# Gated rows turned by VectorE in 32x32 blocks, and down weights in runs of 16 KB

## The chip, the cores and the metric

The kernel runs on one core of a Trainium2 chip. The time is device time in microseconds (us). Three runs of the kernel before took 2269.36, 2270.11 and 2274.81 us; their median, 2270.11 us, is the time before. Engines are called PE (TensorE), DVE (VectorE), ACT (ScalarE), POOL (GpSimd) and SP (SyncE).

## The reference

One decoder layer over 1024 tokens of width 1024, all in float32. A mixer with three branches (a diagonal state-space model, a chunked spatial gating, cross-attention into 256 memory tokens) is followed by a routed mixture of experts, and then a last RMSNorm. The change is in the mixture of experts:

```python
g_idx = argmax(x @ w_group + b_group)            # 1 of 8 groups
top_vals, top_loc = top_k(e_logits[g_idx], 2)    # 2 of the 8 experts in it
# for each expert e, over the tokens that chose it:
y = (silu(xb @ w1[e]) * (xb @ w3[e])) @ w2[e]    # 1024 -> 512 -> 1024
```

There are 64 experts. w1 and w3 of one are 1024x512 (2 MB each), w2 is 512x1024 (2 MB).

## The kernel before

Up to about 1150 us the kernel computes the mixer, the router and a table that lists each expert's tokens. Then comes the expert stage. Its work is cut into units: a unit is up to 32 tokens (CAP) of one expert, and there are 100 of them in this run. `each_unit` (L382) writes the same loop for PE, ACT, DVE and POOL: over 16 turns, over 4 slots, over the units of expert 4t+s. The counts are read from `spans` at run time.

Weights: each of the 4 slots holds one expert, 6 MB. SP loads them in order of experts, all on one queue. `refill` (L548) waits until the last unit of the expert four back has done its gate and up projection (`gu_ready`), then issues the token list (L553), w1 and w3 (`expert_up`, L499; a partition takes 8 rows of 512 numbers that lie side by side, a run of 16 KB), waits for that unit's down projection (`y_ready`), and issues w2 (`expert_down`, L503; a partition takes rows p, 128+p, 256+p and 384+p, four runs of 4 KB each).

A unit u passes through the engines so:

- POOL (`gather`, L685) waits until PE has turned the rows of the unit before, copies 32 indices (L688) and gathers 32 rows of 4 KB from memory into `xg` (L692). There is one `xg`, so there is one gather at a time.
- PE turns the 32 rows (`turn_tokens`, L1031, transposes recorded at L758), DVE copies the result to `xT` (L1710).
- PE does the gate and up projection (L1045, 64 matmuls). The 512 hidden columns are in four quarters of 128: quarter h goes to partitions 32h to 32h+31, so a bank holds 128 partitions (quarter, token) by 128 columns. ACT makes silu of the gate (L1240), DVE multiplies with the up part into `hid` (L1715).
- PE turns the tokens of unit u+1 in between, then `hid` (128x128, L1052), and DVE copies it to `hidT` (L1717).
- PE does the down projection (L1059, 32 matmuls) against `w2s`, ACT drains the result (L1244) and stores it with four DMAs (L1247), 192 packets with their semaphore writes. There is one result row buffer for each slot, so the drain of the next unit in the same slot waits until the last store has landed (L1243).
- ACT's order is silu of u, drain of u, its four DMA issues, silu of u+1.

At the end the results are gathered, two rows for each token, and weighted and normed.

Of the kernel before, what the change touches and what calls it, by code (L numbers as in the profile page):

```python
# [27 lines left out]
ALU = mybir.AluOpType  # L28
# [3 lines left out]
P = 128  # L32
# [22 lines left out]
QUARTERS = P // CAP  # L55
# [48 lines left out]
def program(nc, x, mem, g_mix, g_mem, w_in, w_gate, b_gate, lam_re, lam_im, log_dt, b_re, b_im,  # L104
# [3 lines left out]
    with ctx:  # L108
        def sb(name, shape, dt=F32):
            return ctx.enter_context(nc.sbuf_tensor(name, shape, dt))  # L110

        def sem(name):
            return ctx.enter_context(nc.semaphore(name))


        act_bank = [ctx.enter_context(nc.psum_tensor(f"act_bank{i}", [P, 512], F32)) for i in range(4)]
        dve_bank = [ctx.enter_context(nc.psum_tensor(f"dve_bank{i}", [P, 512], F32)) for i in range(4)]
# [10 lines left out]
        gain_a = sb("gain_a", [P, D])  # L128
# [68 lines left out]
        def tiles(n, k):  # L197
# [16 lines left out]
                  for s in range(2)]  # L214
# [36 lines left out]
        w2s = [b[:, :].rearrange("p (k n) -> p k n", k=4) for b in (unit[7], unit[10], unit[4], rows_store)]  # L251
        FQ, DQ = FF // QUARTERS, D // QUARTERS
        xg = gain_b[0:CAP, :]
        xT = gain_a[:, 0:256].rearrange("p (k t) -> p k t", k=KD)
        silu_g = gain_a[:, 256:384]
        hid = gain_a[:, 384:512]
        hidT = gain_a[:, 512:640].rearrange("p (j t) -> p j t", j=QUARTERS)
        y_rows = [lane_row[:, 0:DQ], lane_row[:, DQ:2 * DQ], now[:, 0:DQ], now[:, DQ:2 * DQ]]
        y_bank = [act_bank[1], act_bank[2], act_bank[3], dve_bank[2]]

# [49 lines left out]
        down_loaded = [sem(f"down_loaded{s}") for s in range(SLOTS)]  # L310
        per_slot = {n: [sem(f"{n}{s}") for s in range(SLOTS)] for n in
                    ("gu_ready", "silu_ready", "hid_ready",
                     "hid_turned", "hidT_ready", "y_ready", "y_drained", "y_stored")}
        picked = [sem(f"picked{b}") for b in range(PICKS)]
        pick_used, out_root, out_rstd, out_scaled = (
            sem("pick_used"), sem("out_root"), sem("out_rstd"), sem("out_scaled"))
# [31 lines left out]
        def glu_job(jobs, name, n):  # L348
            return job(jobs, name, n) if n < 6 else job(jobs, name + "6", n - 6)
# [22 lines left out]
        def logits_job(i):  # L372

            return job(dve_jobs, "out", 4 * i + 4 if i < NT - 1 else 4 * i + 2)

        def rank_job(i):

            return job(dve_jobs, "out", 4 * i + 7 if i < NT - 2 else 29 + 2 * (i - NT + 2))
# [23 lines left out]
        def _(sp):  # L402
# [40 lines left out]
            for s in range(STEP):  # L443
                n = (STEP - s) * GH
# [55 lines left out]
                                 w_up[z].rearrange("e (p k) n -> p (e k n)", p=P)).then_inc(up_loaded[s], 16)  # L500

            def expert_down(w_down, s):
                sp.dma_start(w2s[s], w_down.rearrange("e (k p) n -> p (e k) n", p=P)).then_inc(down_loaded[s], 16)  # L503

            def expert(at):
                return (w1[0][at], w3[0][at]), w2[0][at]
# [12 lines left out]
            for e in range(2):  # L519
                up, down = expert(bass.ds(e, 1))  # L520
                expert_up(up, e)
                expert_down(down, e)

                for i in range(2 + 2 * e, 4 + 2 * e):
                    sp.wait_ge(h_stored[i % 2], 16 * (i // 2))
                    sp.wait_ge(xf_made, i - 1)
                    sp.dma_start(rows_in[i % 2][:, :], x_tiles[i]).then_inc(x_loaded[i % 2], 16)
# [6 lines left out]
            up, down = expert(bass.ds(2, 1))  # L534
            expert_up(up, 2)
            expert_down(down, 2)
            up, down = expert(bass.ds(3, 1))
            expert_up(up, 3, halves=(0,))

            for s in range(2):  # L540
                sp.wait_ge(h_stored[s], 16 * (NT // 2))
                sp.wait_ge(xf_stored[s], 16 * (NT // 2))
            sp.wait_ge(act_filled, jobs_end(act_jobs, "xfT"))
            expert_down(down, 3)
            sp.wait_ge(rows_picked, 1)
            expert_up(up, 3, halves=(1,))
# [190 lines left out]
        def _(pe):  # L737
# [17 lines left out]
            def turn(bank, blocks, rows=P):  # L755

                for n, block_ in enumerate(blocks):
                    ins = nc.tensor.transpose(bank[:, n * rows:(n + 1) * rows], block_, ident[0:rows, 0:rows])  # L758
                return ins
# [172 lines left out]
            for i in range(NT):  # L932
# [7 lines left out]
                z, m = i // KW, i % KW  # L940
# [23 lines left out]
            with pe.Fori(0, KD // 2) as t:  # L964
                for s in range(2):
                    pe.wait_ge(gate_loaded[s], (t + 1) * 96)
                    for z in range(2):
                        cols = slice(z * HALF, (z + 1) * HALF)
                        for i in range(3):
                            n = 6 * s + 3 * z + i  # L970
# [60 lines left out]
            def turn_tokens(u):  # L1031

                pe.wait_ge(tok_gathered, (u + 1) * 16)

                pe.nop(nofuse=True)
                turn(dve_bank[0], [xg[:, k * P:(k + 1) * P] for k in range(KD)], CAP).then_inc(tok_turned, 1)

            def work(c, s, u, t, first):

                pe.wait_ge(xT_ready, u + 1)  # L1040

                pe.wait_ge(up_loaded[s], (t + 1) * UP_INC)
                for k in range(KD):
                    for h in range(QUARTERS):
                        ins = nc.tensor.matmul(  # L1045
                            act_bank[0][h * CAP:(h + 1) * CAP, 0:2 * FQ].rearrange("t (w n) -> t w n", w=2), xT[:, k],
                            w13[s][:, :, k, h * FQ:(h + 1) * FQ], start=k == 0, stop=k == KD - 1)
                ins.then_inc(per_slot["gu_ready"][s], 1)
                turn_tokens(u + 1)

                pe.wait_ge(per_slot["hid_ready"][s], c + 1)
                turn(dve_bank[1], [hid]).then_inc(per_slot["hid_turned"][s], 1)  # L1052
                pe.wait_ge(per_slot["hidT_ready"][s], c + 1)
                pe.wait_ge(down_loaded[s], (t + 1) * 16)

                pe.wait_ge(per_slot["y_drained"][s], c + 1)
                for j in range(QUARTERS):
                    for z in range(QUARTERS):
                        ins = nc.tensor.matmul(y_bank[s][z * CAP:(z + 1) * CAP, 0:DQ], hidT[:, j],  # L1059
                                               w2s[s][:, j, z * DQ:(z + 1) * DQ], start=j == 0, stop=j == QUARTERS - 1)  # L1060
                ins.then_inc(per_slot["y_ready"][s], 1)

            turn_tokens(0)
            each_unit(pe, work)


# [204 lines left out]
        def _(dve):  # L1271
            v = nc.vector
# [236 lines left out]
            for n in range(8):  # L1509
# [4 lines left out]
                m, z = n // 2, n % 2  # L1514
                k = glu_job(dve_jobs, "glu_a", n)
# [68 lines left out]
            with dve.Fori(0, KD // 2) as t:  # L1584
                step.enter(t, 4)
                for s in range(2):
                    for z in range(2):
                        for i in range(3):
                            n = 6 * s + 3 * z + i
# [70 lines left out]
            for i in range(NT):  # L1660
                s = i % 2
# [8 lines left out]
                n = logits_job(i)  # L1670
# [7 lines left out]
            n = rank_job(NT - 1)  # L1678
# [29 lines left out]
            def take_tokens(u):  # L1708
                dve.wait_ge(tok_turned, u + 2)
                v.tensor_copy(xT, dve_bank[0][:, 0:KD * CAP].rearrange("p (k t) -> p k t", k=KD)  # L1710
                              ).then_inc(xT_ready, 1)

            def unit_work(c, s, u, t, first):
                dve.wait_ge(per_slot["silu_ready"][s], c + 1)
                v.tensor_tensor(hid, silu_g, act_bank[0][:, FQ:2 * FQ], ALU.mult).then_inc(per_slot["hid_ready"][s], 1)  # L1715
                dve.wait_ge(per_slot["hid_turned"][s], c + 1)
                v.tensor_copy(hidT, dve_bank[1][:, 0:P].rearrange("p (j t) -> p j t", j=QUARTERS)  # L1717
                              ).then_inc(per_slot["hidT_ready"][s], 1)
                take_tokens(u + 1)

            take_tokens(0)
            each_unit(dve, unit_work)

            def finish(i):
# [43 lines left out]
```

## Time and profile before

| | |
|---|---|
| median of 3 runs | 2270.11 us |
| profiled execution | 2267.0 us |
| its span, first to last instruction | 2265.1 us |
| PE busy (matmul) | 1794.9 us, 79% |
| DVE, ACT, POOL busy | 475.1, 254.8, 258.2 us |
| packets of all DMA queues | 152743, 510.96 MB |
| of these under 8 KB | 135792 |
| granted TensorE clock, mean | 0.908 of full speed |

A busy share is an average over stages with different limits. The DMA share is that of the core's 16 DMA engines, and it can come out a little above 1, since packets overlap at their edges. "Landing" is the time from the issue of a DMA to the last write of its semaphore. Queue q1 is SP's, q10 is ACT's, q0 is POOL's.

### The profile page before, as it was taken

How to read it: one execution, taken by the hardware profiler on the slowest of the kernel's cores; microseconds unless marked ns; L12 is line 12 of the kernel's file. 1: busy time of each engine (PE TensorE's matmuls, PEld its weight loads, DVE VectorE, ACT ScalarE, POOL GpSimd, SP SyncE). 2: the span in 40 equal slices, each digit the busy share in tenths (PEclk: the TensorE clock that was granted, in tenths of full speed). 3: DMA queues.
4: the chain of work that ended last, by engine and by line, in shares of the span. 5: the costliest groups of instructions: out<-in, count | busy, mean ns of one | idle time of the engine just before them, and what ended most of it. 6: DMA issues, size and time to landing. Idle time of an engine off the chain costs nothing.

```text
span 2265.1 us, 38820 instructions
## 1 busy us (share of the span) xinstructions
PE 1794.9 (79%) x13852; PEld 1000.1 (44%) x13853; DVE 475.1 (21%) x1140; ACT 254.8 (11%) x538; POOL 258.2 (11%) x377
## 2 busy tenths in 40 slices
PE   6998999999999999989757777777777776455550
PEld 4655445654444444435434444444444453232220
DVE  6554012431011111025521001010011010000006
ACT  3112212410000000001100000000000000000003
POOL 2940000000000000001111111111111110000014
PEclk9998999999999999999879889899999899676775
DMA  6412013011111110055479999989999979999985
GB/s 224 122 40 107 4 36 105 23 44 42 42 42 42 42 42 29 8 189 197 184 275 400 409 409 406 401 308 374 405 397 369 391 283 419 415 416 420 422 334 210
DMA packets 152743, 510.96 MB, mean 226 GB/s; under 512 B 34352, under 2 KB 84016, under 8 KB 135792
## 3 DMA queue, kind: packets, MB, share of 16 engines
q1 hardware_dynamic: 122096, 461.36, 52.5%
q0 software_dynamic: 8768, 27.02, 3.4%
q10 hardware_dynamic: 21840, 22.06, 2.8%
q8 instruction: 23, 0.38, 0.1%
q14 instruction: 16, 0.13, 0.0%
HBM read 479.71 MB, written 34.35 MB: 227 GB/s over the span
## 4 chain that ended last, share of the span: by engine, by line
PE 56%; DMA 18%; SPq 11%; issue 5%; DVE 5%; ACTq 2%; ACT 1%; POOL 1%; POOLq 0%; DVEq 0%
PE act_bank L751 27%; PE dve_bank L751 14%; DMA gain_b<-xf_rows,gather_idx 11%; SPq L553 5%; PE act_bank L1045 4%; DMA unit_results<-spatialT 3%; SPq L499 3%; PE dve_bank L758 3%; PE act_bank L1059 2%; SPq L503 2%; DMA tokens<-expert_token_table 2%; PE dve_bank L1059 2%; ACTq L1247 1%; DMA unit_results<-lane_row 1%; DVE unit L1311 1%
## 5 line engine op out<-in xcount | busy, mean ns | idle before, releaser
L751 PE MATMUL act_bank<-norm_store,unit 128*128 128x512 f32 x1024 | 448.9, 592 | 0.0
L751 PEld LDWEIGHTS act_bank<-norm_store,unit 128*128 128x128 f32 x1024 | 194.6, 190 | 241.1 <-issue 240.6
L1045 PE MATMUL act_bank<-unit,gain_a 128*32 128x256 f32 x3520 | 207.3, 388 | 26.2 <-issue 26.1
L758 PE MATMUL dve_bank<-ident,gain_b 32*128 32x32 f32 x808 | 73.8, 235 | 179.8 <-DMA gain_b<-xf_rows,gather_idx 179.6
L1059 PE MATMUL act_bank<-unit,gain_a 128*32 128x256 f32 x2208 | 175.4, 471 | 39.6 <-DVE gain_a L1717 39.6
L1715 DVE TENSOR_TENSOR gain_a<-gain_a,act_bank 128x128 f32<-128x128 f32 x100 | 28.8, 288 | 757.0 <-ACT gain_a L1240 739.0
L1045 PEld LDWEIGHTS act_bank<-unit,gain_a 128*32 128x32 f32 x3520 | 123.6, 113 | 111.4 <-issue 53.5
L758 PEld LDWEIGHTS dve_bank<-ident,gain_b 32*128 32x128 f32 x808 | 64.1, 151 | 223.8 <-issue 223.8
L1059 PEld LDWEIGHTS act_bank<-unit,gain_a 128*32 128x32 f32 x2208 | 90.2, 130 | 97.4 <-issue 81.4
L1593 DVE TENSOR_TENSOR rows_store<-dve_bank,rows_store 128x512 f32<-128x512 f32 x48 | 33.2, 692 | 431.1 <-PE dve_bank L751 431.1
L751 PE MATMUL dve_bank<-unit,mid_store 128*128 128x512 f32 x256 | 113.4, 602 | 9.0 <-DMA unit<-in_w_router 9.0
L751 PE MATMUL dve_bank<-unit,unit 128*128 128x512 f32 x256 | 115.1, 592 | 0.0
L688 POOL COPY gather_idx<-tokens 32x1 int32 x100 | 17.8, 178 | 841.7 <-PE dve_bank L758 580.8
L751 PE MATMUL act_bank<-unit,norm_store 128*128 128x512 f32 x256 | 113.5, 603 | 0.0
L751 PE MATMUL dve_bank<-unit 128*128 128x512 f32 (+1 forms) x320 | 104.0, 474 | 6.2 <-ACT unit L1092 6.2
L692 POOL DMA_INDIRECT gain_b<-xf_rows,gather_idx x101 | 94.7, 938 | 83.4 <-POOL gather_idx L688 83.4
L1045 PE MATMUL act_bank<-norm_store,gain_a 128*32 128x256 f32 x1344 | 83.3, 403 | 21.6 <-issue 21.6
L1045 PE MATMUL act_bank<-mid_store,gain_a 128*32 128x256 f32 x1536 | 91.5, 391 | 10.1 <-issue 10.1
L1059 PE MATMUL dve_bank<-rows_store,gain_a 128*32 128x256 f32 x992 | 75.2, 454 | 17.8 <-DVE gain_a L1717 17.8
L751 PEld LDWEIGHTS act_bank<-unit,norm_store 128*128 128x128 f32 x256 | 64.7, 255 | 44.9 <-issue 30.5
L1205 ACT ACTIVATE rows_store<-act_bank,gate_bias_now 128x512 f32<-128x512 f32 x48 | 33.0, 687 | 417.6 <-PE act_bank L751 417.5
L751 PEld LDWEIGHTS dve_bank<-unit,mid_store 128*128 128x128 f32 x256 | 48.9, 193 | 68.9 <-issue 68.9
(227 smaller groups left out, 1474.5 us busy)
## 6 DMA issues: line engine op xcount, KB each, us to landing
unit<-in_w SPq DMA_DIRECT2D x112, 2048.0 KB
norm_store<-in_w SPq DMA_DIRECT2D x32, 2048.0 KB
mid_store<-in_w SPq DMA_DIRECT2D x32, 2048.0 KB
rows_store<-in_w SPq DMA_DIRECT2D x16, 2048.0 KB
unit<-in_w_gate SPq DMA_DIRECT2D x24, 512.0 KB, 5.2
unit<-in_w_in SPq DMA_DIRECT2D x4, 2048.0 KB, 8.9
unit_results<-unit POOLq DMA_DIRECT2D x4, 2048.0 KB, 13.4
unit_results<-spatialT ACTq DMA_DIRECT2D x220, 32.0 KB
```

The costliest lines, as they stand in the source:

```text
L499: sp.dma_start(w13[s][:, z].rearrange("p k n -> p (k n)"), w_up[z].rearrange("e (p k) n -> p (e k n)", p=P)).then_inc(up_loaded[s], 16)
L503: sp.dma_start(w2s[s], w_down.rearrange("e (k p) n -> p (e k) n", p=P)).then_inc(down_loaded[s], 16)
L553: sp.dma_start(tokens[:, s], table_of[bass.ds(e, 1)].rearrange("e p n -> (e p) n")).then_inc(tokens_loaded[s], 16)
L692: pool.indirect_dma_start(xg, None, xf_dram, bass.IndirectOffsetOnAxis(ap=gather_idx[:, 0:1], axis=0), bounds_check=T - 1, oob_is_err=Fals ...
L751: ins = nc.tensor.matmul(out_, stationary, moving, start=first and n == 0, stop=n == len(pairs) - 1)
L758: ins = nc.tensor.transpose(bank[:, n * rows:(n + 1) * rows], block_, ident[0:rows, 0:rows])
L1045: ins = nc.tensor.matmul(act_bank[0][h * CAP:(h + 1) * CAP, 0:2 * FQ].rearrange("t (w n) -> t w n", w=2), xT[:, k], w13[s][:, :, k, h * FQ ...
L1059: ins = nc.tensor.matmul(y_bank[s][z * CAP:(z + 1) * CAP, 0:DQ], hidT[:, j], w2s[s][:, j, z * DQ:(z + 1) * DQ], start=j == 0, stop=j == QU ...
L1205: drained(nc.scalar.activation(gates[n % 4], act_bank[g % 4][:, :], ACT.Sigmoid, bias=gate_bias_now[:, s, i:i + 1]))
L1247: act.dma_start(y_dram[bass.ds(u * CAP, CAP), z * DQ:(z + 1) * DQ], y_rows[s][z * CAP:(z + 1) * CAP]).then_inc(per_slot["y_stored"][s], 16)
L1593: v.tensor_tensor(parts[i], dve_bank[b % 4][:, :], gates[n % 4], ALU.mult).then_inc(dve_drained, 1)
L1715: v.tensor_tensor(hid, silu_g, act_bank[0][:, FQ:2 * FQ], ALU.mult).then_inc(per_slot["hid_ready"][s], 1)
```

## The change

`hid` is still written by DVE, but with its columns in another order: column 4m+k of a quarter goes to place 32k+m. DVE then transposes the whole 128x128 tile in blocks of 32x32. Block (h, k) stays at its place and is transposed inside, so partition 32h+m, columns 32k to 32k+31, hold hidden unit 128h+4m+k of the 32 tokens. That is hidden unit 4p+k for partition p. The down weights are loaded to match it: partition p takes rows 4p to 4p+3 of w2, which lie side by side, one run of 16 KB in place of four of 4 KB. PE's turn of `hid`, the wait for it and its semaphore are gone. DVE waits for its own multiply before the transpose. The down projection's matmuls stay the same.

```diff
--- before.py
+++ after.py
@@ -254,7 +254,9 @@
         xT = gain_a[:, 0:256].rearrange("p (k t) -> p k t", k=KD)
         silu_g = gain_a[:, 256:384]
         hid = gain_a[:, 384:512]
+        hid_blocks = hid.rearrange("p (k m) -> p m k", k=4)
         hidT = gain_a[:, 512:640].rearrange("p (j t) -> p j t", j=QUARTERS)
+        hidT_flat = gain_a[:, 512:640]
         y_rows = [lane_row[:, 0:DQ], lane_row[:, DQ:2 * DQ], now[:, 0:DQ], now[:, DQ:2 * DQ]]
         y_bank = [act_bank[1], act_bank[2], act_bank[3], dve_bank[2]]
 
@@ -310,7 +312,7 @@
         down_loaded = [sem(f"down_loaded{s}") for s in range(SLOTS)]
         per_slot = {n: [sem(f"{n}{s}") for s in range(SLOTS)] for n in
                     ("gu_ready", "silu_ready", "hid_ready",
-                     "hid_turned", "hidT_ready", "y_ready", "y_drained", "y_stored")}
+                     "hidT_ready", "y_ready", "y_drained", "y_stored")}
         picked = [sem(f"picked{b}") for b in range(PICKS)]
         pick_used, out_root, out_rstd, out_scaled = (
             sem("pick_used"), sem("out_root"), sem("out_rstd"), sem("out_scaled"))
@@ -500,7 +502,8 @@
                                  w_up[z].rearrange("e (p k) n -> p (e k n)", p=P)).then_inc(up_loaded[s], 16)
 
             def expert_down(w_down, s):
-                sp.dma_start(w2s[s], w_down.rearrange("e (k p) n -> p (e k) n", p=P)).then_inc(down_loaded[s], 16)
+                sp.dma_start(w2s[s].rearrange("p k n -> p (k n)"), w_down.rearrange("e (p k) n -> p (e k n)", p=P)
+                             ).then_inc(down_loaded[s], 16)
 
             def expert(at):
                 return (w1[0][at], w3[0][at]), w2[0][at]
@@ -1048,8 +1051,6 @@
                 ins.then_inc(per_slot["gu_ready"][s], 1)
                 turn_tokens(u + 1)
 
-                pe.wait_ge(per_slot["hid_ready"][s], c + 1)
-                turn(dve_bank[1], [hid]).then_inc(per_slot["hid_turned"][s], 1)
                 pe.wait_ge(per_slot["hidT_ready"][s], c + 1)
                 pe.wait_ge(down_loaded[s], (t + 1) * 16)
 
@@ -1712,10 +1713,11 @@
 
             def unit_work(c, s, u, t, first):
                 dve.wait_ge(per_slot["silu_ready"][s], c + 1)
-                v.tensor_tensor(hid, silu_g, act_bank[0][:, FQ:2 * FQ], ALU.mult).then_inc(per_slot["hid_ready"][s], 1)
-                dve.wait_ge(per_slot["hid_turned"][s], c + 1)
-                v.tensor_copy(hidT, dve_bank[1][:, 0:P].rearrange("p (j t) -> p j t", j=QUARTERS)
-                              ).then_inc(per_slot["hidT_ready"][s], 1)
+                v.tensor_tensor(hid_blocks, silu_g.rearrange("p (m k) -> p m k", k=4),
+                                act_bank[0][:, FQ:2 * FQ].rearrange("p (m k) -> p m k", k=4), ALU.mult
+                                ).then_inc(per_slot["hid_ready"][s], 1)
+                dve.wait_ge(per_slot["hid_ready"][s], c + 1)
+                v.transpose(hidT_flat, hid).then_inc(per_slot["hidT_ready"][s], 1)
                 take_tokens(u + 1)
 
             take_tokens(0)
```

## Rows read from the trace of the kernel before

**Rows 1.** The page, part 4: share of the ending chain by engine.
```profile
PE 56%; DMA 18%; SPq 11%; issue 5%; DVE 5%; ACTq 2%; ACT 1%; POOL 1%; POOLq 0%; DVEq 0%
```

**Rows 2.** Busy us of each engine by stretch, then granted clock, DMA share, GB/s.
```profile
1155.35:1855.35 700.00, 529.00 (x7940) 322.06 (x7940) 68.75 (x226) 49.63 (x150) 84.76 (x152) 0.92 0.95 375
1855.35:2191.00 335.65, 193.13 (x2480) 106.50 (x2480) 21.86 (x72) 15.88 (x48) 26.77 (x48) 0.78 1.01 414
```

**Rows 3.** Waits, 1155 to 1895 us: engine, line, releaser, total us, times, longest.
```profile
ACT spatialT L1244 <- DMA unit_results<-spatialT: 72.8, 10, 9.5
...
PE dve_bank L758 <- DMA gain_b<-xf_rows,gather_idx: 48.8, 43, 2.6
...
ACT lane_row L1244 <- DMA unit_results<-lane_row: 33.1, 5, 8.8
```

**Rows 4.** Waits, 1895 to 2200 us.
```profile
POOL gather_idx L688 <- DMA tokens<-expert_token_table: 248.4, 18, 14.1
```

**Rows 5.** Chain of waits, 1895 to 2200 us: start us, us, what.
```profile
2141.10 34.24 DMA tokens<-expert_token_table
```

**Rows 6.** Instructions by line: busy us, mean ns, idle before.
```profile
L758 PE MATMUL dve_bank<-ident,gain_a 128*128 128x128 f32 x100 | 36.5, 365 | 36.4 <-DVE gain_a L1715 31.4 <-issue 2.5
L1717 DVE COPY gain_a<-dve_bank 128x128 f32<-128x128 f32 x100 | 29.2, 292 | 192.0 <-PE dve_bank L758 191.4 <-issue 0.6
L1715 DVE TENSOR_TENSOR gain_a<-gain_a,act_bank 128x128 f32<-128x128 f32 x100 | 28.8, 288 | 757.0 <-ACT gain_a L1240 739.0 <-issue 18.0
...
L1466 DVE TENSOR_TENSOR_SCAN unit<-unit,unit 128x128 f32<-128x128 f32 x32 | 15.3, 480 | 1.1
```

**Rows 7.** Timeline of PE: start us, us, what, idle before it.
```profile
1589.48 0.65 PE L758 MATMUL dve_bank<-ident,gain_b 32*128 32x32 f32 x8 [1.83 <-DMA gain_b<-xf_rows,gather_idx]
...
1590.96 1.93 PE L1059 MATMUL act_bank<-unit,gain_a 128*32 128x256 f32 x32 [0.57 <-DVE gain_a L1717]
```

**Rows 8.** Timeline of POOL: issues of the gather.
```profile
1574.14 0.94 POOL L692 DMA_INDIRECT gain_b<-xf_rows,gather_idx  x1 [0.83 <-POOL gather_idx L688]
...
1582.52 0.94 POOL L692 DMA_INDIRECT gain_b<-xf_rows,gather_idx  x1 [0.82 <-POOL gather_idx L688]
...
1591.38 0.94 POOL L692 DMA_INDIRECT gain_b<-xf_rows,gather_idx  x1 [0.82 <-POOL gather_idx L688]
```

**Rows 9.** Gathers issued at 1574.14, 1582.52, 1599.76 us; all from 1160 to 1895 us.
```profile
DMA to landing us min/median/max: 6.0/6.0/6.0
...
DMA to landing us min/median/max: 6.8/6.8/6.8
...
DMA to landing us min/median/max: 7.2/7.2/7.2
...
DMA to landing us min/median/max: 2.4/6.8/8.0
```

**Rows 10.** DMA packets from 1577.9 to 1579.9 us and from 1586.5 to 1589.2 us.
```profile
DMA packets 188, 0.68 MB, mean 338 GB/s; under 512 B 23, under 2 KB 23, under 8 KB 188
...
DMA packets 112, 0.84 MB, mean 311 GB/s; under 512 B 32, under 2 KB 37, under 8 KB 69
```

**Rows 11.** ACT's queue (q10), 1658 to 1664 and 1666 to 1672 us; timeline of ACT.
```profile
q10 hardware_dynamic: 225, 0.15, 7.8%
...
q10 hardware_dynamic: 89, 0.07, 3.3%
...
1312.35 1.76 ACTq L1247 DMA_DIRECT2D unit_results<-spatialT  x4
...
1324.18 0.38 ACT L1244 ACTIVATE spatialT<-act_bank 128x256 f32<-128x256 f32 x1 [9.45 <-DMA unit_results<-spatialT]
...
1328.68 0.28 ACT L1240 ACTIVATE gain_a<-act_bank 128x128 f32<-128x128 f32 x1 [4.11 <-issue]
```

**Rows 12.** The weights' queue (q1): 1178 to 1182 us, then 1876 to 1884 us.
```profile
q1 hardware_dynamic: 385, 1.58, 97.4%
...
q1 hardware_dynamic: 231, 3.24, 95.1%
```

## Prediction

> **What bounds the kernel now.** I read the page first, then the busy time by stretch, the waits of the expert stage, its chain, and last the timelines around one unit. The page's chain is PE for 56%, DMA for 18% and SP's queue for 11% [rows 1]. The change touches only the expert stage, from about 1155 us on. It has two halves. From 1155.35 to 1855.35 us the 16 DMA engines are busy for 0.95 of the time; from 1855.35 to 2191 us for 1.01 [rows 2]. The share looks alike, the limit is not. In the first half (75 units, experts with up to five units) no engine waits for a DMA of weights. What waits for a DMA is PE for the gathered rows, 43 times, and ACT for an older store of results, 15 times [rows 3]. In the second half (one unit for each expert) POOL waits 18 times, 248.4 us, for a token list that stands in SP's queue behind the weights [rows 4], and the last list takes 34.24 us from its issue to its landing [rows 5]. So the first half runs at the pace of a loop of gather, PE and ACT, and the second at the pace of the weight loads.
>
> The loop of the first half: PE turns the gathered rows of unit u+1, POOL is released, copies the indices and issues the next gather, it lands, PE turns again. Issues at 1582.52 and 1591.38 us are 8.86 us apart [rows 8] with a landing of 6.8 us [rows 9], so 2.06 us of the cycle are not the DMA. A landing of 6.0 us would allow 8.06 us, but the issues at 1574.14 and 1582.52 us are 8.38 us apart: there PE came 0.3 us later than the gather and set the pace.
>
> **Part 1, the turn on DVE.** Now DVE multiplies (288 ns), PE turns (365 ns), DVE copies (292 ns) [rows 6], and the down projection starts 0.57 us after PE's turn [rows 7]. Afterwards DVE multiplies with a strided output and transposes in place of the copy. The trace has no such transpose. Below stands nothing under the 288 ns of an operation of this size, since copy, reduce and multiply of 128x128 all take about that; above stands the scan, 480 ns [rows 6]. I take 0.29 us, nearest to the copy, and nothing for the stride. Gone is PE's turn between the two, and I set the hand-over to PE and back against DVE's new wait on its own semaphore. So 0.36 us leave the chain of a unit; the bounds are 0.17 (a transpose of 480 ns) and, with the hand-overs gone too, a little over 0.4. Where PE sat waiting for the gather it is more: the turn of the hidden rows comes after the token turn in PE's order, so from 1589.48 to 1590.96 us 1.48 us pass up to the down projection [rows 7]; later the transposed rows are ready and only the token turn's 0.65 us and a start remain, about 0.75 us saved. That is PE time in a cycle where PE then waits for the next gather, so it is worth nothing by itself; it is slack. It counts in some 17 of the 75 cycles (seven with the DMA engines quiet, ten behind a late ACT): 17 x 0.36 = 6 us less. DVE queues the next token copy behind the wait; PE needs it only after the down projection.
>
> The Trainium skill ("VectorE: DVE Perf Modes", The three transpose paths) gives 311 ns for a 128x128 bf16 transpose in 32x32 blocks. No row here shows one; as an estimate by that page the saving would be 0.34 us a unit, and the sum 0.3 us worse.
>
> **Part 2, down weights in runs of 16 KB.** A load of 2 MB goes from 512 runs to 128. In a stretch of runs of 4 KB, the queue of weights moved 1.58 MB in 97.4% of 16 x 4 us, 25.4 KB/us for each engine; in one of 16 KB runs 3.24 MB in 95.1% of 16 x 8 us, 26.6 KB/us [rows 12]. For 131 KB on each engine this is 5.16 against 4.93 us, 0.23 us for each load. Only the second half is paid by it: 21 loads x 0.23 = 4.8 us less. Bounds: nothing saved (the two rates are from short stretches beside other traffic), and 0.35 us a load, 7 us.
>
> The Trainium skill ("DMA: Bandwidth & Descriptors", Why small descriptors are slow) speaks of some 3 bus cycles for each packet and calls joining worth it only up to 256 B. As an estimate by that page the gain would be under 2% of a load, 2 us over the second half in place of 4.8; the rows speak for more.
>
> The other side of long runs: the gathers (4 KB runs) and the result stores (1 KB runs) share the engines with the weights. Between 1577.9 and 1579.9 us all 188 packets are under 8 KB, the down load is passing, and the gather issued at 1574.14 us lands in 6.0 us. Between 1586.5 and 1589.2 us 43 of 112 packets are 16 KB runs of an up load, and the gather issued at 1582.52 us takes 6.8 us, one at 1599.76 us 7.2 us [rows 9, 10]. With nothing else moving it is 2.4 us. So a small packet waits for the run ahead of it, and the length of that run is what the change makes four times longer. Of the 80 gathers up to 1895 us, 25 land beside 4 KB runs in a cycle under 9.1 us (8.3 to 8.4 us mostly). At a landing of 7.1 us their cycle becomes 2.06 + 7.1 = 9.16 us: +0.75 us each, 19 us. A slower loop leaves more quiet time, which gives back perhaps 4 us. I take +15 us; bounds 0 (slack covers all of it) and +22.
>
> Stores suffer in the same way. In 6 us beside 4 KB runs 225 packets of ACT's queue are through, in 6 us beside 16 KB runs 89 [rows 11]; a store has 192. ACT drains the next unit of the same expert only after the last store: at 1324.18 us it had waited 9.45 us for that [rows 11], and PE behind it stood still, since the next silu comes after in ACT's order. A store that meets a down load would take some 3 to 4 us longer. Some 25 drains have such a store before them, but PE has gained 0.75 us of slack a unit and most delays end in a wait for the gather. I take a third of 25 x 1.7 us, 14 us, less 8 us for the slack: +6 us; bounds -5 and +30 (ACT in step with the stores in every expert of several units).
>
> **Sum.** Against the profiled execution (2267.0 us, its span 2265.1 and 1.9 around it): first half -6 + 15 + 6 = +15 us; second half -4.8, and 1 us from the shorter last unit: -6. Together +9 or so: 2276. The median of the runs is 3.1 us above the profiled execution, so the forecast is 2280 us (2279 rounded up, because PE's clock tends to fall after longer waits: the second half has 0.78 against 0.92 [rows 2]).
>
> **Rivals.**
> A. Faster: the gather beside down loads stays near 6 us. Then the 25 cycles that PE sets fall from 8.4 to 8.06 us, where the gather takes over (-9 us), the stalls behind ACT shorten (-6), and the second half gives -6: 2270 - 21 = 2249 us. It decides if the landing beside the new down loads is under 6.3 us. For it: landings vary, and only a few packets of a gather meet a long run. Against it: rows 9 pair off cleanly with rows 10. A weaker form, in which the DMA engines' 16 KB runs were split, is excluded by the up loads, which already move in such runs.
> B. It cancels: PE's new slack takes the store delays and half of the gather's, +8 in the first half, -6 in the second: 2272 us. For it: the gains and losses are of one size. Against: the gather cycle has no slack of its own.
> C. Much slower: store waits chain through ACT. The store issued from 1312.35 us held the drain until 1324.18 us, 12 us after the drain before it, and the next silu came 4.5 us later, at 1328.68 us [rows 11]; DVE and the down projection add 3 us up to the next drain. A pair of units then costs 12.1 + 7.5 = 19.6 us in place of two gather cycles, 18.3; over 17 pairs 22 us, and the experts of three and more half as much again: 2270 + 33 - 6 = 2297 us. Against it: the DMA engines rest longer when the loop is slower, and stores are then quick.
>
> **How the numbers follow.** Forecast 0.50 (own range 2273 to 2288), A 0.20, B 0.20, C 0.10. A measurement of this kernel tells about 0.3% from no change, 6.8 us. Slower (over 2276.9): 0.38 of the forecast's 0.50, all of C, a little of B: 0.50. Same: the forecast's rest and most of B: 0.28. Faster: A and a little of B: 0.22. The range is 2255 to 2295: it leaves out the lower part of A and C's upper part.
>
> **What would show it.** In the profile after: no PE turn of the hidden rows, DVE's transpose near 0.29 us, the down projection under 0.8 us after the token turn where PE waited; packets 24,500 to 25,000 fewer; landings of gathers at 6.8 to 7.2 us in all busy stretches (under 6.3 us proves A); PE's waits for the gather longer than the 48.8 us of now; ACT's waits for stores more than 15 (unchanged is B, doubled is C); the stretch up to the refill of expert 43 longer than 700 us, and the 21 loads behind it 5 us shorter. Were PE found waiting for weights in the first half, the whole argument would be wrong.

## The result and the profile after

| | before | after |
|---|---|---|
| median of 14 runs each | 2269.61 us | 2283.80 us (2276.00 to 2286.73) |
| ratio, 95% interval | | 1.0057 [1.0046, 1.0067] |
| profiled execution, its span | 2267.0, 2265.1 us | 2282.96, 2281.0 us |
| first half (75 units, up to the refill of expert 43) | 700.0 us | 720.95 us |
| second half (21 loads) | 335.65 us | 329.70 us |

The change makes the kernel 13 us slower (0.57% of 2269.6), where 10 us were forecast. The changed kernel's page, part 4 (the chain that ended last, by engine), and its packet line:

```profile
PE 54%; DMA 30%; DVE 5%; issue 4%; ACTq 4%; ACT 2%; POOL 1%; SPq 1%; POOLq 1%; DVEq 0%
...
DMA packets 128168, 510.96 MB, mean 224 GB/s; under 512 B 34353, under 2 KB 84017, under 8 KB 103025
```

Against [rows 1], DMA rises from 18% of the chain to 30%, and SP's queue falls from 11% to 1%. There are 24575 packets fewer. So the down loads did become long runs. Next the two halves, in the columns of [rows 2]: start and end, length, busy us of PE, its weight loads, DVE, ACT and POOL, granted clock, DMA share, GB/s.

```profile
1155.35:1876.30 720.95, 524.64 (x7872) 307.64 (x7872) 79.39 (x226) 49.52 (x150) 84.45 (x152) 0.89 0.92 364
1876.30:2206.00 329.70, 187.87 (x2456) 99.29 (x2452) 26.33 (x72) 15.85 (x48) 26.66 (x48) 0.77 1.00 419
```

The first half is 21 us longer with the DMA engines *less* busy (0.92 in place of 0.95): it isn't bandwidth that ran short. The second half, which waits for weights, is 6 us shorter, at 419 in place of 414 GB/s. The waits of the changed kernel from 1157 to 1916 us, then the one of POOL from 1916 to 2215 us (engine, tile, line, releaser, total us, times, longest):

```profile
PE dve_bank L761 <- DMA gain_b<-xf_rows,gather_idx: 101.4, 57, 3.8
ACT spatialT L1245 <- DMA unit_results<-spatialT: 97.0, 12, 9.7
...
ACT lane_row L1245 <- DMA unit_results<-lane_row: 31.1, 4, 8.7
...
POOL gather_idx L691 <- DMA tokens<-expert_token_table: 244.3, 18, 13.9
```

Against [rows 3], PE's wait for the gathered rows has doubled from 48.8 us; ACT's wait for stores grew from 105.9 us in 15 waits to 128.1 us in 16. No engine waits for weights in the first half, after as before. All gathers issued from 1160 to 1916 us, to compare with the last line of [rows 9]:

```profile
DMA to landing us min/median/max: 2.4/7.2/9.3
```

The median went from 6.8 to 7.2 us and the longest from 8.0 to 9.3 us. DVE by line (busy us, mean ns, idle before it), 1155 to 2215 us:

```profile
L1711 DVE COPY gain_a<-dve_bank 128x256 f32<-128x256 f32 x101 | 41.4, 410 | 181.6 <-PE dve_bank L761 181.5
L1716 DVE TENSOR_TENSOR gain_a<-gain_a,act_bank 128x128 f32<-128x128 f32 x100 | 37.1, 371 | 774.8 <-ACT gain_a L1241 750.6 <-issue 24.2
L1720 DVE STREAM_TRANSPOSE gain_a<-gain_a 128x128 f32<-128x128 f32 x100 | 31.2, 312 | 3.4
```

The block transpose takes 312 ns, close to the copy that it replaces (292 ns [rows 6]). The multiply with its strided, interleaved operands takes 371 ns in place of 288 ns. (The Trainium skill, "VectorE: DVE Perf Modes", The three transpose paths, gives 311 ns for bf16; the trace, which has float32, shows 312 ns.) PE's timeline of the changed kernel around two waits for a gather (start us, us, what, idle before):

```profile
1600.53 0.65 PE L761 MATMUL dve_bank<-ident,gain_b 32*128 32x32 f32 x8 [2.25 <-DMA gain_b<-xf_rows,gather_idx]
1601.11 3.58 PE L1060 MATMUL act_bank<-unit,gain_a 128*32 128x256 f32 x32
...
1637.61 0.65 PE L761 MATMUL dve_bank<-ident,gain_b 32*128 32x32 f32 x8 [3.72 <-DMA gain_b<-xf_rows,gather_idx]
1638.19 3.13 PE L1060 MATMUL dve_bank<-rows_store,gain_a 128*32 128x256 f32 x32
```

Two things are to be seen. The down projection starts 0.58 us after the token turn, where it was 1.48 us [rows 7]: the transposed rows lie ready. But the same 32 matmuls now take 3.58 and 3.13 us, where the one in [rows 7] took 1.93. The granted clock of the changed kernel says why; stretches before the wait, of the two down projections, and of one at 1647.5 us (columns as above, the clock is the third number from the end):

```profile
1594.00:1600.00 6.00, 4.28 (x80) 2.80 (x72) 0.68 (x2) 0.66 (x2) 0.00 (x0) 1.00 1.02 380
1601.10:1604.70 3.60, 3.59 (x34) 1.47 (x32) 0.42 (x1) 0.00 (x0) 1.11 (x2) 0.53 1.04 434
1638.20:1641.30 3.10, 3.10 (x33) 1.27 (x32) 0.42 (x1) 0.00 (x0) 1.11 (x2) 0.59 1.00 428
1647.50:1649.50 2.00, 2.00 (x39) 1.23 (x41) 0.42 (x1) 0.00 (x0) 0.76 (x2) 1.00 0.98 412
```

After PE idled 2.25 and 3.72 us, its clock was granted at 0.53 and 0.59 of full speed (1.2 GHz for most of the stretch, out of 2.4), and at 1.00 after a wait of 1.33 us. The last wait alone does not decide it: a group of the changed kernel at 1736.21 us took 1.93 us behind a wait of 2.98 us. Counted in the timelines of the first half, 24 of 75 groups of 32 took more than 2.5 us before, and 34 of 75 after. PE by line in the first half, the kernel before and then the changed one (busy us, mean ns of one, idle before it):

```profile
L1059 PE MATMUL act_bank<-unit,gain_a 128*32 128x256 f32 x1632 | 119.4, 441 | 29.2 <-DVE gain_a L1717 29.2
L1059 PE MATMUL dve_bank<-rows_store,gain_a 128*32 128x256 f32 x768 | 55.3, 436 | 13.8 <-DVE gain_a L1717 13.8
...
L758 PE MATMUL dve_bank<-ident,gain_a 128*128 128x128 f32 x75 | 25.7, 342 | 35.3 <-DVE gain_a L1715 30.7 <-issue 2.5
```

```profile
L1060 PE MATMUL act_bank<-unit,gain_a 128*32 128x256 f32 x1632 | 128.2, 467 | 39.0 <-DVE gain_a L1720 38.6
...
L1060 PE MATMUL dve_bank<-rows_store,gain_a 128*32 128x256 f32 x768 | 62.8, 482 | 22.7 <-DVE gain_a L1720 22.7
```

The change takes 25.7 us of turning from PE, and the same 2400 matmuls of the down projection take 191.0 us in place of 174.7: 16 us of it are lost again to the lower clock.

### The profile page after: what moved, and what is told of

It reads as the page before. It is cut to its first block, busy times and chain, and to the rows that moved or that the text cites. A ratio compares the mean times of both kernels' runs of the same rounds, so it can differ in the third digit from the quotient of the medians.

```text
span 2281.0 us, 38620 instructions
## 1 busy us (share of the span) xinstructions
PE 1781.1 (78%) x13752; PEld 975.2 (43%) x13753; DVE 490.5 (22%) x1140; ACT 254.6 (11%) x538; POOL 257.0 (11%) x377
## 4 chain that ended last, share of the span: by engine, by line
PE 54%; DMA 30%; DVE 5%; issue 4%; ACTq 4%; ACT 2%; POOL 1%; SPq 1%; POOLq 1%; DVEq 0%
PE act_bank L754 26%; PE dve_bank L754 14%; DMA gain_b<-xf_rows,gather_idx 12%; DMA tokens<-expert_token_table 10%; DMA unit_results<-spatialT 5%; PE act_bank L1048 3%; PE act_bank L1060 3%; ACTq L1248 2%; PE dve_bank L761 2%; PE dve_bank L1060 2%; DMA unit_results<-lane_row 2%; DVE unit L1312 1%; PE act_bank L922 1%; PE dve_bank L952 1%; PE dve_bank L796 0%
## 5 line engine op out<-in xcount | busy, mean ns | idle before, releaser
L1048 PE MATMUL act_bank<-unit,gain_a 128*32 128x256 f32 x3520 | 216.1, 400 | 20.1 <-issue 19.5
L1060 PE MATMUL act_bank<-unit,gain_a 128*32 128x256 f32 x2208 | 186.4, 495 | 39.7 <-DVE gain_a L1720 39.2
L1716 DVE TENSOR_TENSOR gain_a<-gain_a,act_bank 128x128 f32<-128x128 f32 x100 | 37.1, 371 | 774.8 <-ACT gain_a L1241 750.6
L1048 PEld LDWEIGHTS act_bank<-unit,gain_a 128*32 128x32 f32 x3520 | 122.3, 117 | 119.7 <-issue 60.6
L1060 PEld LDWEIGHTS act_bank<-unit,gain_a 128*32 128x32 f32 x2208 | 85.8, 135 | 100.2 <-issue 81.8
L1060 PE MATMUL dve_bank<-rows_store,gain_a 128*32 128x256 f32 x992 | 82.9, 491 | 25.0 <-DVE gain_a L1720 25.0
L1048 PE MATMUL act_bank<-norm_store,gain_a 128*32 128x256 f32 x1344 | 78.5, 386 | 18.6 <-issue 18.6
L1711 DVE COPY gain_a<-dve_bank 128x256 f32<-128x256 f32 x101 | 41.4, 410 | 181.6 <-PE dve_bank L761 181.5
```

Source lines behind the costliest of these rows:

```text
L1048: ins = nc.tensor.matmul(act_bank[0][h * CAP:(h + 1) * CAP, 0:2 * FQ].rearrange("t (w n) -> t w n", w=2), xT[:, k], w13[s][:, :, k, h * FQ ...
L1716: v.tensor_tensor(hid_blocks, silu_g.rearrange("p (m k) -> p m k", k=4), act_bank[0][:, FQ:2 * FQ].rearrange("p (m k) -> p m k", k=4), ALU ...
```

## The experiments

All ran beside the kernel before, which had medians of 2267.3 to 2270.2 us. Loads in shorter runs are issued as two DMAs of half the bytes, so that their access patterns keep the same number of dimensions. The edits are shown shortened: semaphore increments, and the counts that PE waits for, are left out. Ratios carry their 95% interval; for microseconds I multiply by 2269.6.

### One part at a time

e2_runs_only: the kernel before with the long runs alone. What it computes is not the layer, since the rows of w2 no longer match the hidden columns; the work is the same.

```diff
-sp.dma_start(w2s[s], w_down.rearrange("e (k p) n -> p (e k) n", p=P))
+sp.dma_start(w2s[s].rearrange("p k n -> p (k n)"), w_down.rearrange("e (p k) n -> p (e k n)", p=P))
```

> The kernel before with its turn on PE, only the down load in 16 KB runs. The down weights' rows then do not match the hidden columns, so the output is not the layer's; the work and its order are the same. Theory T: gathers land in about 7.1 us everywhere, the first half grows by 20 us or a little more than in the changed kernel (no slack from DVE's turn), the second half shrinks by 5 us: 2288 us (2281 to 2296), slower than the changed kernel. Rival D: close to before, 2262 to 2270 us.

Measured: 2299.60 us, 1.0132 [1.0110, 1.0154], **+30 us**, above its range of 2281 to 2296 us. Its gathers (1160 to 1930 us), then its waits (1157 to 1930 us):

```profile
DMA to landing us min/median/max: 2.4/7.1/9.2
```

```profile
ACT spatialT L1245 <- DMA unit_results<-spatialT: 89.8, 11, 9.7
PE dve_bank L759 <- DMA gain_b<-xf_rows,gather_idx: 56.2, 47, 3.3
ACT lane_row L1245 <- DMA unit_results<-lane_row: 24.2, 3, 9.1
```

e1b_turn_only: the changed kernel with its down loads back in runs of 4 KB (partition p still takes rows 4p to 4p+3).

```diff
-sp.dma_start(w2s[s].rearrange("p k n -> p (k n)"), w_down.rearrange("e (p k) n -> p (e k n)", p=P)
+for b in range(2):
+    sp.dma_start(w2s[s].rearrange("p (a b) n -> p b a n", b=2)[:, b],
+                 w_down.rearrange("e (p a b) n -> b p (e a) n", p=P, b=2)[b]
```

> DVE's block transpose as in the changed kernel, but the down weights in runs of 4 KB, as two loads of 1 MB, each with every second row of a partition's four. Theory T (long runs of weights delay gathers and stores): gathers beside down loads land in 5.8 to 6.2 us again, and the kernel is faster than before, about 2260 us (2250 to 2266), since DVE's turn shortens a unit's chain and gives PE slack. Rival D (DVE's turn itself costs, through the 371 ns multiply or the order on DVE): 2270 us or more.

Measured: 2260.95 us, 0.9956 [0.9940, 0.9972], **-10 us**, as expected. Its gathers (1160 to 1885 us) and waits (1157 to 1885 us):

```profile
DMA to landing us min/median/max: 2.4/6.8/8.3
```

```profile
ACT spatialT L1247 <- DMA unit_results<-spatialT: 87.0, 12, 9.8
PE dve_bank L763 <- DMA gain_b<-xf_rows,gather_idx: 81.4, 54, 3.5
ACT lane_row L1247 <- DMA unit_results<-lane_row: 53.1, 9, 8.8
```

What follows: the two parts have opposite signs. One path from the kernel before to the changed one has a single down DMA at every step: the long runs cost 30 us (e2), and the turn then gives back 17 us (1.0132 less 1.0057, times 2269.6). The other path goes by e1b, with two down DMAs in place of one: -10 us, and then +23 (1.0057 less 0.9956). What the second DMA does by itself is in both of these numbers, and no run takes it out. The landing tells which part does what: 6.8 us at the median with 4 KB down loads, as before, and 7.1 to 7.2 with 16 KB, whoever turns the rows. PE's wait for the gather also grows in e1b, where the time falls, and so does ACT's wait for stores (140.1 us in 21 waits), while e2, the slowest, has 114.0 us in 14. What e1b's engines wait for is slack, not loss. A wait grows both when what is awaited comes later and when the waiting engine comes earlier; only the landing tells them apart.

### All weights in short runs

If long runs delay the gathers, the gate and up loads, in 16 KB runs before and after, do it too. e3b_all_4k has the DVE turn and 4 KB runs everywhere; e4_old_turn_4k the same loads with PE's turn; e6_up2k as e3b, but gate and up loads in runs of 2 KB. The gate and up loads of e3b:

```diff
-sp.dma_start(w13[s][:, z].rearrange("p k n -> p (k n)"), w_up[z].rearrange("e (p k) n -> p (e k n)", p=P))
+for b in range(2):
+    sp.dma_start(w13[s][:, z].rearrange("p (a b r) n -> p b a (r n)", b=2, r=2)[:, b],
+                 w_up[z].rearrange("e (p a b r) n -> b p (e a) (r n)", p=P, b=2, r=2)[b])
```

> As e1b_turn_only, and w1 and w3 in runs of 4 KB too, each as two loads of 1 MB. Theory T: all gathers land near 5.9 us and all stores in 6.5 to 7.5 us, so most of the 15 waits for stores vanish; the first half goes from 700 us to about 640 us at cycles of 8.0 to 8.3 us, the second half grows by 21 x 0.46 = 10 us: 2220 us (2205 to 2240). Rival E (what delays a gather is how busy the engines are, not the length of a run): 2270 us or more, since only the loads change, and for the slower.

> The kernel before, PE's turn kept, only w1 and w3 in runs of 4 KB as two loads each (the down weights have 4 KB already). Theory T: gathers near 5.9 us, but PE's chain (8.4 us a new expert, 7.0 us within one) now sets more cycles than the gather: first half about 650 us, 2230 us in all (2215 to 2250), 5 to 15 us slower than e3b_all_4k, which is what DVE's turn is then worth. Rival E: about 2280 us.

> As e3b_all_4k, but w1 and w3 in runs of 2 KB. Theory T: gathers 0.3 to 0.5 us quicker again, which is worth little once PE's chain sets the pace (-5 us in the first half), while ACT's 1 KB packets move 21.7 KB/us for each engine against 25.4 in 4 KB runs, so 2 KB runs should cost 4% of the 4 MB of each expert in the second half, 21 x 0.4 = 8 us: 2225 us (2205 to 2245), no better than e3b_all_4k. Rival E: over 2280 us.

| | median | ratio |
|---|---|---|
| e3b_all_4k | 2250.11 us | 0.9915 [0.9902, 0.9928] |
| e4_old_turn_4k | 2252.04 us | 0.9924 [0.9910, 0.9937] |
| e6_up2k | 2278.95 us | 1.0041 [1.0029, 1.0053] |

e3b is 19 us faster than before, but 30 slower than expected; e4 is 22 and e6 54 us above its forecast. The page of e3b (the chain), its gathers (1160 to 1850 us), its waits (1157 to 1850 us) and its busy time from 1155 us, in the columns of [rows 2]:

```profile
PE 47%; SPq 41%; DVE 4%; issue 4%; DMA 3%; ACT 1%; ACTq 0%; POOL 0%; POOLq 0%; DVEq 0%
```

```profile
DMA to landing us min/median/max: 5.3/5.9/7.9
```

```profile
POOL gather_idx L695 <- DMA tokens<-expert_token_table: 105.1, 10, 14.9
PE dve_bank L765 <- DMA gain_b<-xf_rows,gather_idx: 88.7, 50, 9.6
...
ACT spatialT L1249 <- DMA unit_results<-spatialT: 31.8, 9, 4.1
ACT lane_row L1249 <- DMA unit_results<-lane_row: 25.0, 7, 3.9
```

```profile
1155.00:1820.00 665.00, 501.54 (x7921) 302.75 (x7923) 80.59 (x229) 50.31 (x152) 85.89 (x154) 0.93 1.01 390
1820.00:2149.00 329.00, 176.53 (x2244) 91.68 (x2236) 23.75 (x65) 14.18 (x43) 23.41 (x42) 0.73 1.03 402
```

The mechanism held: gathers land in 5.9 us at the median, and the longest wait of ACT for a store is 4.1 us in place of 9.7. What I missed is what comes late next. The first half now fills the DMA engines (share 1.01), the token lists stand in SP's queue behind weights already there (POOL waits for one 10 times), and SP's queue takes the share of the chain that DMA had. The weight stream is the bound of both halves, and at 402 GB/s it is slower than the 419 of 16 KB runs. That fits e4 too: its gathers land in 5.9 us as well and its chain is the same, and with the stream as bound the DVE turn is worth 2 us, which the intervals don't tell from nothing, not the 5 to 15 expected. The queue of SP shows the change of regime. First the changed kernel's waits of SP's queue, 1155 to 2215 us, then e3b's:

```profile
SPq L556 <- PE act_bank L1048: 488.4, 48, 40.2
```

```profile
SPq L560 <- PE act_bank L1052: 21.1, 3, 15.8
```

SP waited 48 times for a unit to free a slot, and in e3b 3 times. e6 lost its gain to the stream as well: with 2 KB runs in two thirds of it the stream moved 377 GB/s from 1155 to 1820 us, in place of e3b's 390, and 390 in place of 402 from 1820 to 2149 us. The quicker gathers that it was to bring did not come: 5.9 us at the median, as in e3b. (The Trainium skill, "DMA: Bandwidth & Descriptors", Why small descriptors are slow, says that joining neighbouring descriptors into one packet is only worth it up to 256 B. The runs here make the descriptors themselves longer, and they still gain above that size: 402, 414 and 420 GB/s with 4, 8 and 16 KB, in stretches with the engines full.)

### What the stores carry

Two kernels leave three quarters of the result stores out, one from each version: e11_after_quarter from the changed one, e12_before_quarter from the one before.

```diff
-for z in range(QUARTERS):   # stores of a drained unit, ACT
+for z in range(1):
```

> The changed kernel, but ACT stores only the first of a unit's four quarters (three quarters of the results are left out; the result buffer is cleared ahead in the mixer instead), so a store has 48 packets and not 192, and ACT issues one DMA and not four. It tells apart what the long runs do through the stores (S) and through the gathers (T2). If the stores carry most of the loss, this kernel and e12_before_quarter are within 8 us of each other. If the gathers carry most of it, the changed kernel stays 10 us or more slower in this pair too, and its expert stage gains as much from the missing stores as the one of before does, some 15 to 25 us. I hold T2 the likelier: this kernel 2262 us (2245 to 2275).

> The kernel before with the same three quarters of the stores left out: the partner of e11_after_quarter. T2: 2248 us (2235 to 2262), 10 us or more below e11_after_quarter. S: within 8 us of it.

Measured: e11 2250.33 us, 0.9922 [0.9906, 0.9937]; e12 2243.18 us, 0.9894 [0.9877, 0.9911]. Without most stores the change still costs 7 us between the medians (6 by the ratios), against 14 with them. PE's waits for the gather in e11 (1157 to 1900 us) and in e12 (1157 to 1880 us); ACT has no wait for a store in either:

```profile
PE dve_bank L761 <- DMA gain_b<-xf_rows,gather_idx: 128.1, 71, 3.9
```

```profile
PE dve_bank L758 <- DMA gain_b<-xf_rows,gather_idx: 66.0, 51, 2.7
```

Both times lie in their ranges, but the difference was to be 10 us or more if the gathers carry most of the loss, and under 8 us if the stores do. At 7 us it falls on the side of the stores, against what I held likelier. It is not enough to decide: each ratio is known to 0.15%, 3 to 4 us, so the share by stores lies anywhere from a little to nearly all, and half and half is no more than the middle of it. The split between stores and gathers stays open.

### Runs of 8 KB

e7_all_8k: the DVE turn, and every weight load in runs of 8 KB.

```diff
+for b in range(2):
+    sp.dma_start(w13[s][:, z].rearrange("p (b a) n -> p b (a n)", b=2)[:, b],
+                 w_up[z].rearrange("e (p b a) n -> b p (e a n)", p=P, b=2)[b])
+# w2s in the same way
```

> DVE's turn and all expert weights in runs of 8 KB (each load as two of half a run). In e3b_all_4k the gathers were quick and the weight queue itself became the bound over the whole stage at 397 GB/s. Theory T': run length trades the one for the other; with 8 KB the queue moves some 2% more and the gathers land in 6.2 to 6.5 us: 2243 us (2232 to 2256), at or below e3b_all_4k. Rival: no middle, at 8 KB a gather already waits like at 16 KB and the time is over 2265 us.

Measured: **2231.86 us, 0.9836 [0.9823, 0.9849]**, the fastest of all, 37 us under before and 50 under the changed kernel. e3b has the same number of DMAs and the same rows in each partition, so the 18 us between e3b and e7 are the length of the runs alone. Its page (the chain), its gathers (1160 to 1850 us) and its busy time:

```profile
PE 51%; SPq 19%; DMA 13%; DVE 5%; issue 5%; ACTq 4%; ACT 2%; POOL 0%; POOLq 0%; DVEq 0%
```

```profile
DMA to landing us min/median/max: 5.5/6.3/8.0
```

```profile
1155.00:1820.00 665.00, 507.69 (x7864) 308.57 (x7864) 77.72 (x225) 49.65 (x150) 84.58 (x151) 0.92 1.00 395
1820.00:2149.00 329.00, 184.66 (x2396) 97.55 (x2396) 25.70 (x71) 15.51 (x47) 25.64 (x46) 0.76 1.01 414
```

The gathers land in 6.3 us, between 5.9 and 7.2, and the stream moves 414 GB/s, between 402 and 420. It keeps most of both.

e8_down8k puts 8 KB runs in the down loads alone (two DMAs), with the 16 KB gate and up loads of before. It was to tell whether e1b's gain over the changed kernel is from short runs or only from two DMAs in place of one.

> The changed kernel (DVE's turn, w1 and w3 in runs of 16 KB) with the down weights in runs of 8 KB, as two loads: the step between e1b_turn_only (4 KB, 2261 us) and the changed kernel (16 KB, 2284 us). Theory T: the landings of gathers and stores beside down loads grow with the length of a run, so this lies between the two, 2270 us (2264 to 2279). Rival (two loads of 1 MB in place of one are what made e1b_turn_only fast, not the short runs): the same as e1b_turn_only, 2261 us or less.

Measured: 2261.48 us, 0.9972 [0.9962, 0.9982], below its range of 2264 to 2279 us. By the ratios it is 4 us slower than e1b and 19 faster than the changed kernel, and the intervals of e8 and e1b overlap. The rival (two DMAs, whatever the run) gave this time, so the total doesn't exclude it. The landings do not follow the number of DMAs. I sorted the gathers by the mean packet of SP's queue in the 3.5 us before they land. Beside 4 KB runs they take 5.95 us on average with one down DMA (the kernel before, 23 gathers) and 6.1 with two (e1b, 25). Beside 8 KB runs they take 6.5 us (e8, 29), and beside 16 KB runs 7.1 to 7.3 (before, changed, e1b, e2 and e8). That follows the run; a separate share of the two DMAs in the time stays open. What excludes DMA count as the whole cause: the kernel before has one down DMA in 4 KB runs, e2 one in 16 KB runs, and that pair differs by 30 us.

### Short runs first, long runs later

The first half wants short runs and the second a fast stream, so three kernels switch at expert 40.

```diff
-with sp.Fori(1, TURNS) as t:
-    for s in range(SLOTS):
-        refill(t * SLOTS + s, s)
+for a, b, runs in ((1, 10, 4), (10, TURNS, 16)):   # e14: (1, 10, 8)
+    with sp.Fori(a, b) as t:
+        for s in range(SLOTS):
+            refill(t * SLOTS + s, s, runs)
```

e9_split loads the 16 KB part in two DMAs of 64 partitions each; e9b_split_4_16 and e14_split_8_16 in one DMA of 128 partitions, with a second semaphore increment by SP.

> DVE's turn; weights of experts 4 to 39 (1 to 5 units each) in runs of 4 KB, those of experts 40 to 63 (1 unit each) in runs of 16 KB. Theory T': each half gets the run length that its own bound wants. The last unit of expert 39 is done near 1805 us (1855 before), then 21 loads follow at 15.6 us: 2218 us (2208 to 2235), the fastest of all. Rival: the gain of the first half is given back, since the loads of the second half are what the stage waits for in either case: 2245 us or more.

> e9_split again, but the 16 KB runs of experts 40 to 63 are loads over all 128 partitions, as in the changed kernel. In e9_split loads over 64 partitions each moved only 230 GB/s. Theory T': first half as in e3b_all_4k (gather cycles near 8.1 us, weight queue near its limit), 651 us; second half 330 us as in the changed kernel: 2226 us (2214 to 2238). Rival (the slowness of e9_split came from the change of run length itself): over 2300 us.

> As e9b_split_4_16, but the first experts in runs of 8 KB, as in e7_all_8k, whose first half took 659 us and whose queue moved 402 GB/s. Second half 4 us below e7_all_8k: 2228 us (2220 to 2236), level with e9b_split_4_16. If the weight queue is what bounds e9b_split_4_16's first half, this kernel is the faster; if the gathers, the slower.

e9_split took 2555.07 us at the median of 6 runs, from 2360.07 to 2606.66, where 2218 was forecast; the runs spread too far for a ratio. Its busy time in the profiled run (2529.12 us), in a stretch of 4 KB runs and one of 64-partition loads, and then e9b's:

```profile
1155.00:1750.00 595.00, 436.09 (x6833) 260.63 (x6833) 69.35 (x196) 43.01 (x130) 74.79 (x134) 0.90 1.01 383
1900.00:2350.00 450.00, 156.03 (x1864) 79.45 (x1864) 20.39 (x56) 12.19 (x37) 18.00 (x33) 0.65 1.01 239
```

```profile
1155.00:1820.00 665.00, 497.79 (x7800) 299.17 (x7802) 80.07 (x226) 49.14 (x149) 84.46 (x152) 0.92 1.01 391
1820.00:2149.00 329.00, 190.61 (x2472) 101.00 (x2463) 24.95 (x70) 15.86 (x48) 25.40 (x46) 0.76 1.01 420
```

Loads of 64 partitions moved 239 GB/s in that run with the DMA engines busy all the time; the same bytes over 128 partitions move 420, in a kernel that switches run length at the same expert. So the switch is not what made e9_split slow; why half the partitions are so much slower stays open. e9b took 2235.56 us, 0.9859 [0.9843, 0.9875], inside its range; e14 2239.42 us, 0.9879 [0.9863, 0.9894], above its range of 2220 to 2236. The intervals of the two overlap, so they don't tell which limit e9b's first half has. Neither beats e7's plain 8 KB. e9b's first half moves 391 GB/s with the engines full, where e7's moves 395: the 4 KB runs are the slower stream there too. e14 has e7's first half, and a faster second one (424 GB/s in place of 417 from 1900 to 2140 us, some 4 us), yet it takes 8 us more. The traces show a likely reason. Just behind the switch, from 1800 to 1820 and 1820 to 1840 us, its DMA share is 0.67 and 0.52, and that of e7 0.82 and 0.96: some 12 us of stream are lost there, while SP waits for units to free the slots (58.4 us of such waits end from 1790 to 1850 us, and 34.2 us in e7).

## Why the prediction was right, and where its sizes were off

The sign, the mechanism and the total held: 2280 us forecast, 2283.8 measured, inside the range. The terms were less exact than their sum.

- **The turn on DVE, forecast -7 us (-6, and -1 in the last unit).** e1b, with two down DMAs, measures -10 us [-14, -6]; from e2 to the changed kernel it is -17. The prices of DVE were too low: 312 ns for the transpose and 371 for the multiply, together 103 ns more than the copy and the multiply of [rows 6]. "Nothing for the stride" was wrong by 83 ns. The down projection does start under 0.8 us after the token turn (0.58), as forecast.
- **The long runs, forecast +16 us (+15 gathers, +6 stores, -5 stream).** This is the term that was mis-sized: +23 us beside the DVE turn, +30 without it. The gathers did move to the time forecast (7.2 us at the median). But in the changed kernel the 61 beside 16 KB runs take 7.3 us on average where 7.1 was priced, the longest, 9.3 us, exceed anything that I had priced, and the priced sum took 25 cycles only. Of the stores, "a third of 25" was +14 less 8 of slack; e11 and e12 leave their share anywhere from a little to nearly all, so no run confirms the +6, nor the +15 beside it.
- **The lower clock was left out of the first half.** I reckoned it at 1 us, in the second half. 34 groups of 32 matmuls at over 2.5 us in place of 24, 16 us more for the same down projections, and a granted clock of 0.89 over the first half in place of 0.92, go with the longer waits of PE. How much of the 21 us this is, the runs do not separate. It does not make a kernel slower by itself: from 1155 to 1855 us e1b and e2 both have 0.89, and one is 10 us faster than before, the other 30 slower.
- **The parts may not add.** -10 and +30 would make +20; together they make +13. That fits the forecast, which had charged 8 us of slack that PE gets from the turn and that takes up part of what the long runs delay. But the 7 us have the errors of three ratios in them, together some 7 us, and e1b's second DMA, so the slack is not shown.
- **The second half, forecast -6 us:** 335.65 to 329.70 us, -6.
- **The halves against each other:** the first was to be +15 and is +21.

The rivals. A (2249 us, landings under 6.3 us) is excluded by the landing of 7.2 us. B (2272 us, cancels) is excluded by the interval, whose lower end is 2280 us, though its sign was there: ACT's waits for stores are 16 where they were 15. C (2297 us, stores in step with ACT) needed the number of those waits doubled. Whether it has a true piece is open: ACT does wait longer for stores, 128.1 in place of 105.9 us, but it waits longer still in e1b, 140.1 us, and e1b is faster than before.

## What to carry to other kernels

Where a saturating stream and small, awaited transfers share the DMA engines, the run length of the stream is a setting with two sides: longer runs raise its rate a little (402, 414, 420 GB/s with 4, 8, 16 KB) and delay each small transfer more (5.9, 6.3 us, and 7.2 with 16 KB). Ask of each stage which of the two it waits for, and try the middle: here 8 KB everywhere, with the turn on DVE, was worth 37 us where the change lost 13. And time two edits of one change apart: this one held a gain of 17 us under a loss of 30.

## What the hardware showed unexpectedly

- A DVE multiply of 128x128 float32 with operands in interleaved order took 371 ns in place of 288.
- Loads of 64 partitions in 16 KB runs moved 239 GB/s at a DMA share of 1.01 in the profiled run of e9_split, against 420 for 128 partitions in e9b; the time also spread by 10% between runs.
- 32 matmuls took 1.93 us at a granted clock of 1.00 and 3.1 to 3.6 us at 0.53 to 0.59, after PE had idled for 2.25 and 3.72 us. With 1.33 us of idling the clock stayed at 1.00, and once with 2.98 us too.
